# Decoder block on eight cores: the planner that orders the instructions gets other durations for ACT, DVE and PE work and for waits between engines

## The reference, cut to what matters

```python
h = rms_norm(x, norm_mix_pre)                      # (2048, 1024) on each core
z = h @ w_in                                       # u | v | q | k | v_attn | gate_a | gate_b
y_a = chunked_spatial_gating(gelu(u_a), gelu(v_a), w_s, b_s, ln_v_g, ln_v_b)
# 16 heads of 64, each under three causal windows (window, dilation):
# (128, 1), (512, 4), (2048, 16), ALiBi bias, merged by their softmax denominators
y_b = dilated_attention_mixture(q * 0.125, k, v_b)
merged = sigmoid(g_a + b_a) * (y_a @ w_a_proj) + sigmoid(g_b + b_b) * (y_b @ w_b_proj)
x = x + rms_norm(merged @ w_out, norm_mix_post)
h = rms_norm(x, norm_ffn_pre)
f = square(relu(h @ w_ff1)) @ w_ff2                # 1024 -> 4096 -> 1024
out = x + rms_norm(f, norm_ffn_post)
```

## Time and profile before

| | us |
|---|---|
| median of 3 runs | 1183.62 |
| lowest and highest | 1182.1 and 1188.18 |
| profiled execution: its time | 1182.13 |
| profiled execution: span of the slowest core | 1180.6 |
| spans of the eight cores | 1175.9 to 1180.6 |
| granted TensorE clock, mean of each core | 0.986 to 0.990 of full speed |

### The profile page before, as it was taken

One profiled execution on the slowest core, in us unless ns is written; L12 is line 12 of the kernel. 1 busy time (PEld: TensorE's weight loads), 2 busy tenths in 40 slices (PEclk: granted clock), 3 DMA queues, 4 the chain that ended last, 5 costly groups with the idle time before them and its releaser, 6 DMA issues.

```text
span 1180.6 us, 20834 instructions; the slowest of 8 cores (1175.9 to 1180.6 us)
## 1 busy us (share of the span) xinstructions
PE 1111.3 (94%) x7304; PEld 564.6 (48%) x7304; DVE 740.1 (63%) x1224; ACT 530.0 (45%) x771; POOL 145.5 (12%) x259
## 2 busy tenths in 40 slices
PE   4899999999798999999999999889999999999996
PEld 2566555665455445444444444444444444444442
DVE  5767677777756643755544457877783258774417
ACT  4567787778857663121122135563331023332021
POOL 3301000001011431000000012530000031000002
PEclk9999999999989999999999999989999999999998
DMA  8679868779603409877677879954456459648433
GB/s 225 183 160 154 150 140 148 157 136 156 116 18 76 64 9 128 109 212 194 178 186 203 207 234 282 313 194 155 153 185 226 153 186 294 198 137 265 158 108 143
DMA packets 95336, 197.55 MB, mean 167 GB/s; under 512 B 39169, under 2 KB 55681, under 8 KB 90370
## 3 DMA queue, kind: packets, MB, share of 16 engines
q1 hardware_dynamic: 86082, 154.28, 42.3%
q0 software_dynamic: 9152, 41.95, 23.1%
HBM read 194.11 MB, written 56.62 MB: 212 GB/s over the span
## 4 chain that ended last, share of the span: by engine, by line
PE 82%; ACT 5%; issue 4%; DVE 4%; DMA 3%; POOL 2%; DVEq 0%; SPq 0%; ACTq 0%; POOLq 0%
PE pst L195 82%; ACT sb_Et L643 2%; DMA sb_xt<-x 2%; DMA sb_wva<-w_va 1%; ACT sb_Lr L714 1%; PE pst L199 1%; DVE sb_hx L1203 1%; POOL sb_st L1000 1%; POOL sb_st L1002 1%; DVE sb_tp L1012 0%; DVE sb_sn L1201 0%; DVE sb_PT L655 0%; DVE sb_xo L1014 0%; ACT sb_junk L1186 0%; ACT sb_junk L1016 0%
## 5 line engine op out<-in xcount | busy, mean ns | idle before, releaser
L643 ACT ACTIVATE sb_Et<-pst 128x1024 bf16<-128x1024 f32 (+1 forms) x160 | 150.3, 973 | 34.1 <-PE pst L195 18.8
L195 PE MATMUL pst<-sb_r,sb_hid 128*128 128x512 bf16 x640 | 139.1, 379 | 0.0
L655 DVE TENSOR_TENSOR sb_PT<-sb_Et,sb_EB 128x1024 bf16<-128x1024 bf16 (+2 forms) x200 | 110.4, 569 | 39.2 <-ACT sb_Et L643 26.1
L195 PE MATMUL pst<-sb_hT,sb_wqk 128*128 128x512 bf16 x512 | 124.7, 389 | 7.5 <-ACT sb_hT L504 7.5
L195 PE MATMUL pst<-sb_merged,sb_r 128*128 128x512 bf16 x512 | 121.8, 380 | 2.0 <-DVE sb_tp L1012 2.0
L950 ACT ACTIVATE sb_sg<-pst,sb_small 128x512 f32<-128x512 f32 x64 | 44.0, 687 | 172.8 <-PE pst L195 105.5
L195 PE MATMUL pst<-sb_hT,sb_wg 128*128 128x512 bf16 x512 | 116.7, 379 | 0.0
L1096 ACT ACTIVATE sb_sn<-pst 128x512 f32<-128x512 f32 x96 | 57.0, 597 | 106.3 <-PE pst L195 105.8
L195 PEld LDWEIGHTS pst<-sb_r,sb_hid 128*128 128x128 bf16 x640 | 62.6, 98 | 75.5
L195 PE MATMUL pst<-sb_TB,sb_r 128*128 128x512 bf16 x384 | 94.3, 383 | 0.3 <-DVE sb_hid L1099 0.3
L195 PEld LDWEIGHTS pst<-sb_merged,sb_r 128*128 128x128 bf16 x512 | 50.0, 98 | 62.5 <-issue 2.8
(11 more groups left out here) (118 smaller groups left out, 1600.7 us busy)
## 6 DMA issues: line engine op xcount, KB each, us to landing
w_bf<-w POOLq DMA_DIRECT2D x32, 512.0 KB, 9.2
sb_PB<-w_bf SPq DMA_DIRECT2D x32, 512.0 KB, 6.5
w_comb<-sb_PB SPq DMA_DIRECT2D x32, 512.0 KB, 6.9
sb_r<-w_comb SPq DMA_DIRECT2D x32, 512.0 KB, 3.6
sb_r<-w_comb SPq DMA_DIRECT2D x16, 1024.0 KB, 5.2
sb_r<-w_bf SPq DMA_DIRECT2D x32, 384.0 KB, 3.6
sb_r<-w_bf SPq DMA_DIRECT2D x12, 1024.0 KB, 5.1
sb_xt<-x SPq DMA_DIRECT2D x16, 512.0 KB, 14.0
```

What stands on the lines that cost most here:

```text
L195: e.matmul(out, lhsT=l, rhs=r, start=st, stop=sp, skip_group_check=True))
L643: P.act(lambda e: e.activation(out=et[:, :, 0:W], in_=psall[:, sb:sb + 2, 0:W], func=AF.Exp, scale=0.125), 2 * W, [], [et.key()], [sb, sb ...
L655: P.dve(lambda e: e.tensor_tensor(out=o, in0=i0, in1=i1, op=ALU.mult), n, rk, [pt.key()], rate=2, name="mask")
```

## The change

Only numbers of the planner change: the cost of a matmul has a lower floor and no longer assumes that the score matmuls (64 rows, `slow`) take 0.55 of their columns' time, ACT and DVE operations get a larger fixed part and a lower or higher rate, and the handover to another engine goes from 0.08 to 0.2 us, the one on the same engine from 0.02 to 0.05. A 1024-element exp goes from 0.963 to 0.977 us, a 512-element DVE operation out of PSUM from 0.623 to 0.689, a score job of four 256-column matmuls from 0.240 to 0.371.

```diff
@@ def pe
-            cost += max(n / 2400.0 + 0.0025, 0.055) * (0.55 if slow else 1.0)
+            cost += max(n / 2400.0 + 0.0025, 0.050) * (0.85 if slow else 1.0)
@@ def act
-        return self._add("act", [fn], (0.4 if acc else 0.11) + n / 1200.0, ..., lat=0.04, name=name)
+        return self._add("act", [fn], (0.45 if acc else 0.23) + n / 1370.0, ..., lat=0.02, name=name)
@@ def dve
-        return self._add("dve", [fn], 0.09 + n / (960.0 * rate), ...,
+        return self._add("dve", [fn], 0.1 + n / (870.0 * rate), ...,
@@ def schedule
-                    a = o.end + (0.08 if s.eng != o.eng or o.nb else 0.02)
+                    a = o.end + (0.2 if s.eng != o.eng or o.nb else 0.05)
```

More of the change, by code:

```diff
@@ L202, in act @@
     def act(self, fn, n, reads, writes, banks=(), prio=None, name="", acc=False):
-        return self._add("act", [fn], (0.4 if acc else 0.11) + n / 1200.0, reads, list(writes) + [self.bank(b) for b in banks], prio, lat=0.04, name=name)
+        return self._add("act", [fn], (0.45 if acc else 0.23) + n / 1370.0, reads, list(writes) + [self.bank(b) for b in banks], prio, lat=0.02, name=name)
     def dve(self, fn, n, reads, writes, banks=(), prio=None, name="", rate=1):
-        return self._add("dve", [fn], 0.09 + n / (960.0 * rate), reads, list(writes) + [self.bank(b) for b in banks], prio,
+        return self._add("dve", [fn], 0.1 + n / (870.0 * rate), reads, list(writes) + [self.bank(b) for b in banks], prio,
                          lat=0.04, name=name)
```

## The result

The changed kernel takes 1172.9 us (median of 4 runs, 1171.1 to 1173.0), the kernel before on the same chip 1184.2 (1182.1 to 1188.2). The ratio is 0.989, 95% interval 0.986 to 0.992. The forecast was no visible change. Now and then an execution of either kernel runs some per cent longer with the cores of one die at a lower granted clock; the medians and ratios here leave those out.

A forecast was written before the change was run, and what follows sets the result against it. PE, busy 1111.3 of 1180.6 us, was taken as the bound, leaving only its waits. Terms -3.0 + 1.8 + 1.5 - 1.7 + 1.0 summed to -0.4 us, giving 1182 us, no visible change; range 1173 to 1190.

The forecast's parts named there:

- What bounds the kernel: Whole kernel: PE busy 1111.3 of 1180.6 us; its waits in attention, at wva and in the output projection are left.
- Attention, pairs 1 to 5: Pair changes up to 312 us: four clusters of exp waits vanish (5.8 us), new ybT waits take back 2.6; -3.0 us.
- The wait for wva: Start of the wva matmuls: the last quarter lands after 13 us, PE stands 10.9 us, not 9.1; +1.8 us.
- formula L - 2.1: At wva: PE's standing time in us, L being the last quarter's time to landing, with 3.3 us of PE work.
- Behind that wait: After PE restarts at wva: ACT's work is level with PE's, one cluster of waits returns; +1.5 us, bounds 0 and +3.4.
- hTc: PE's 3.2 us wait for POOL's copy at 381 us: a u-branch group now stands in front; -1.7 us.
- tmpm: End of the gating: the last wait of 1.8 us gets one more group in its chain; +1.0 us.
- Output projection: Output projection: the 5.6 us of waits for tp can shrink or grow by half; 0, bounds -3 and +3.
- The clock: Behind the wva wait: TensorE at half its clock costs about 2 us, left equal on both sides.
- B: Rival, handovers pay off: clusters go, wva lands in 8.4 us, output projection gains; about -11.8 us, 1171; chance 0.25.
- D: Rival, pairs 4 and 6: EB issued behind V comes late, DVE holds masks 3.6 us in two pairs; +7, 1190; chance 0.08.
- C: Rival, stop at wva grows: V loads and EB overtake its last quarter; 1189.5 at L = 17.4, 1191 at 19; chance 0.12.

The follow-up runs named there:

- e11: Changed kernel with gfin's multiplication 80 places later and the weight conversion on POOL put behind wva's last quarter: 1171.2 us, ratio 0.990 to the kernel before.
- e8: Changed kernel with EB of pairs 2 to 7 issued ahead of V and gfin's multiplication 80 places later: 1171.7 us, ratio 0.991 to the kernel before.
- e9: Changed kernel with wva's last quarter held until the last pv2 of pair 5, behind V's loads: 1184.4 us, ratio 1.002 to the kernel before.
- e5: Kernel before with the planner's new numbers only from the output projection on, FFN included: 1175.2 us, ratio 0.994.
- e10: The changed kernel run again unaltered, on the chip of the later runs: 1172.4 us, ratio 0.990 to the kernel before.
- e3: Kernel before with the planner's new numbers only up to the end of attention, old ones behind: 1187.0 us, ratio 1.003.
- e6: Changed kernel with EB of pairs 2 to 7 issued ahead of V's loads: 1172.4 us, ratio 0.992 to the kernel before.
- e12: Changed kernel with gfin's multiplication later, the conversion behind wva, and EB of pairs 4 and 6 ahead of V: 1169.1 us, ratio 0.987 to the kernel before.

## Why the prediction was wrong

*What bounds the kernel* held: PE's waits in three places, and nothing to win behind 880 us. The sum of -0.4 us failed in nearly all its terms; attention and wva make 8.1 of the 9.1 us of idle time between forecast and measurement, and the errors of the others, of 0.2 to 2.6 us, pull both ways and leave 1.0. The range was missed by 0.1 us, but the forecast, no visible change, was wrong by its mechanism.

- *Attention, pairs 1 to 5* (-3.0): the direction and the mechanism held, waits of 8.7 us in 18 became 4.7 in 12 (two of them, 1.34 and 1.04 us, stand behind the last projection and are not of this stage), but hardly anything came in their place. I took 2.6 us back for waits for ybT behind each change of pair; from 86 to 312 us the changed kernel waits for ybT 0.2 us. Idle time fell by 6.3 us. "The middle of gain and take-back" should have been the full gain of 5.8.
- *The wait for wva* (+1.8): the step that failed most. "I take 13, near the two that share the engines with V, since most of its flight lies beside the V loads." It doesn't. V's first load goes out 4.0 to 9.7 us behind wva, by which time more than half of the flight is over on seven of the eight cores. On core 7 hardly any V is beside it and the landing is the longest, 10.0 us; POOL, SP and the landing:

```profile
298.67 0.52 POOL L597 DMA_DIRECT2D w_bf<-w  x1 [6.03 <-PE pst L195]
...
301.01 0.56 POOL L780 DMA_DIRECT2D sb_wva<-w_va  x1 [0.79 <-PE pst L195]
```
```profile
310.71 2.19 SPq L585 DMA_DIRECT2D sb_V<-v_scr  x4
```
```profile
sb_wva<-w_va POOLq DMA_DIRECT2D x1, 512.0 KB, 10.0
```

It landed after 8.7 us (median). The row that fitted was the 8.4 us of two such DMAs issued 2.2 us apart without a V load, and what made it long was, by e11, the conversion ahead of it: 5.5 us there, with that conversion behind it and V still 4 us behind. With the formula L - 2.1 PE would stand for 6.6; it stood for 4.6, for its work there took longer than my 3.3 us, on core 4 with 3.26 us for a class that takes 1.86 at full clock. The order of issue had to be turned into times before a row was picked. The Trainium skill's estimate of 4.4 us ("DMA: Bandwidth & Descriptors", section "Anatomy of one DMA") is below every such landing in these traces; the shortest of them all took 4.9 us (e8, core 6, at 492 us). But "the shortest of such DMAs here took 5.8 us" was wrong too: in the kernel before, a conversion at 499 us landed after 5.0. That the place is worth this much was seen rightly: e9 makes 14 us out of it.

- *Behind that wait* (+1.5): right in kind, too small. Idle time there rose by 3.8, a little over the bound of 3.4.
- *hTc* (-1.7): the wait of 3.2 us went, but one of 3.8 us for ybT took its place, at the first matmuls on wu; the stage won 0.9 us of idle time.
- *tmpm* (+1.0): did not come. 2.9 us in 3 waits and not 2.6 in 2, and the stage is 0.3 better.
- *Output projection* (0, bounds -3 and +3): idle time -2.6, and by the estimate above another 3.2 us of half clock in the changed kernel; e5, which has the FFN's new numbers too, wins 7.3. Half of the 5.6 us for tp went, which was the bound and should have been costed from the move of the transposes.
- *The clock*, left "equal on both sides" at wva and out of the sum elsewhere, was not equal: about 0.9 of the 11.3 - 9.5 = 1.8 us that idle time doesn't explain.

Of the rivals, B came true: the clusters gone, wva after 8.7 us (8.4 in its working), output projection -2.6 (-1.5). Its -11.8 us lie 0.5 from the 11.3 measured, and that is in part luck: it left out the 3.8 us that came behind the wait, and the larger gains in the output projection, in attention and by the clock made up for them. D came true on single cores, at little cost to the changed kernel: its median core is 11.8 us faster in e10, its time 11.1. In e3 and e11 it cost more. It had 0.08 because I asked whether EB is late on average (3 us in hand) and not on the worst of eight cores. C did not happen; e9 shows that a longer stop there costs the whole gain.

## What to carry to other kernels

Where a planner's costs move a load against others, put the issue times on one axis and ask what is already in flight when it goes out, and what joins it during its flight; a row for a crowded neighbourhood prices the load only if the neighbours are there. On eight cores a load with little slack must be judged by its worst core, and a change to the order by the median core too, for one late load hides it (e3, e11): moving one ahead (EB) is worth nothing if it then flies beside the next that is on the path (wva). And compare stages by idle time and by the clock granted in them, for an order that moves work over their borders makes their lengths meaningless.

## What was not expected of the hardware

The same load in the same order differs widely between cores and runs. The last quarter of wva took 5.1 to 5.7 us on five cores of e11, with a conversion issued 0.5 us behind it and V from about 4 us behind, and up to 13.4 in e6, with the conversion 2.3 us and one load of EB of 320 KB 1.7 us ahead of it and V again 4 to 5 us behind. By the medians, what stood ahead of the load counted and what followed it hardly; single cores broke that both ways, with 8.2 us on core 1 of e12 and 5.3 on core 2 of e9, where V had gone out first. EB behind V usually landed in time, and once made DVE wait 13.0 us. What decides which core is late was not found.
